# Sixteen first tiles and fifteen routing-query tiles as three products of rounded parts, and the router's gate shares taken between its index sums

## What is computed

```
# first stack, each layer l
h = rms_norm(x, attn_norm_g[l])
proj = h @ w_in[l]                    # 8932 columns: attention, rwkv, pool, retention, gates
r, wd, k, v, ad, gd = split_cols(token_shift(pb, mu), B_COLS)   # rwkv columns of proj
y = pooled(pc) @ pool_w                # pool columns of proj
...
x = x + square(relu(h2 @ mlp_up[l])) @ mlp_down[l]

# second stack, each layer l, after its mixer: PEER experts
q  = (h @ peer_w_q[l])                 # 2048 columns, 8 heads of 2 x 128
s  = q . sub_keys                      # 128 scores for each half of each head
top 16 of each half, top 16 of the 256 sums: the experts of a token and head
shares = softmax(the 16 sums)
out = sum over chosen experts of share * gelu(h . u_e) * v_e
```

## Time and profile before

| | |
|---|---|
| median of 3 runs | 4067.25 us (4060.14 to 4067.51) |
| the profiled execution's own time | 4059.76 us |
| its span, first to last instruction | 4057.9 us |
| PE busy | 96% of the span |
| DVE, ACT, POOL busy | 53%, 36%, 9% |
| mean granted clock of PE | 0.968 of full speed |

### The profile page before, as it was taken

The page is one execution under the profiler, slowest core; times in us unless marked ns, Lnnn a source line. Parts: engine busy times, 40 slices in busy tenths (PEclk is TensorE's granted clock), DMA queues, the critical chain, the costliest instruction groups (busy, mean ns, idle before and its releaser), DMA issues.

```text
span 4057.9 us, 65583 instructions
## 1 busy us (share of the span) xinstructions
PE 3881.6 (96%) x23880; PEld 3474.5 (86%) x23880; DVE 2157.3 (53%) x4800; ACT 1465.2 (36%) x3010; POOL 345.1 (9%) x468
## 2 busy tenths in 40 slices
PE   8999999999999999978999999999989999999999
PEld 6888889989888898776888989889878889898988
DVE  1345337523344474632697555555433985555555
ACT  2122126321211463212344444444432344444444
POOL 4001100040011000000044000000000270000000
PEclk9999999999899998978999999999999999999999
DMA  5552248654422585402423455555443325555453
GB/s 145 130 161 63 63 133 264 207 139 129 118 66 63 172 263 170 114 26 78 122 85 131 167 172 171 168 172 174 121 115 113 117 92 174 171 169 174 166 175 122
DMA packets 595489, 565.53 MB, mean 139 GB/s; under 512 B 56523, under 2 KB 520410, under 8 KB 594906
## 3 DMA queue, kind: packets, MB, share of 16 engines
q1 hardware_dynamic: 594660, 559.59, 45.5%
q0 software_dynamic: 352, 3.15, 0.2%
q10 hardware_dynamic: 278, 0.08, 0.0%
HBM read 553.30 MB, written 9.44 MB: 139 GB/s over the span
## 4 chain that ended last, share of the span: by engine, by line
PE 92%; DVE 5%; ACT 2%; issue 1%; SPq 0%; DMA 0%; DVEq 0%; ACTq 0%
PE bank L733 22%; PE bank L1187 14%; PE bank L753 10%; PE bank L1201 6%; PE bank L1202 6%; PE bank L1200 6%; PE bank L1139 5%; PE bank L1176 4%; PE bank L1154 3%; PE bank L729 2%; PE bank L822 1%; PE bank L1129 1%; PE bank L935 1%; PE bank L945 1%; PE bank L933 1%; PE bank L778 1%
## 5 line engine op out<-in xcount | busy, mean ns | idle before, releaser
L733 PE MATMUL bank<-hT,ring 128*128 128x256 f32 (+1 forms) x3184 | 716.6, 385 | 21.5 <-ACT hT L1426 16.2
L733 PEld LDWEIGHTS bank<-hT,ring 128*128 128x128 f32 (+1 forms) x3184 | 606.4, 191 | 115.7 <-issue 26.1
L1187 PE MATMUL bank<-h_high,u_parts 128*128 128x256 f32 x3072 | 437.9, 285 | 0.0
L2682 DVE TENSOR_TENSOR u_parts<-bank,u_parts 128x512 fp32r<-128x512 f32 x384 | 247.1, 685 | 328.4 <-ACT u_parts L1720 328.4
L1200 PE MATMUL bank<-v_high,w_low 128*128 128x512 f32 x1024 | 406.8, 397 | 0.4 <-DVE v_low L2703 0.4
L1201 PE MATMUL bank<-v_low,w_high 128*128 128x512 f32 x1024 | 406.1, 397 | 0.0
L1202 PE MATMUL bank<-v_high,w_high 128*128 128x512 f32 x1024 | 405.0, 396 | 0.0
L1187 PEld LDWEIGHTS bank<-h_high,u_parts 128*128 128x128 f32 x3072 | 395.5, 189 | 5.9
L1416 ACT ACTIVATE arena<-bank 128x256 f32<-128x256 f32 (+2 forms) x326 | 124.7, 386 | 684.5 <-PE bank L733 518.2
L2703 DVE TENSOR_TENSOR v_low<-ring,v_high 128x512 fp32r<-128x512 f32 x512 | 336.9, 689 | 65.5 <-ACT v_high L1737 41.3
L1720 ACT ACTIVATE u_parts<-bank 128x512 fp32r<-128x512 f32 x384 | 207.2, 591 | 352.8 <-PE bank L1187 347.0
(11 more groups left out here) (398 smaller groups left out, 5940.3 us busy)
## 6 DMA issues: line engine op xcount, KB each, us to landing
ring<-in_peer_u SPq DMA_DIRECT2D x256, 512.0 KB, 4.2
ring<-in_peer_v SPq DMA_DIRECT2D x256, 512.0 KB, 3.5
ring<-in_w_in SPq DMA_DIRECT2D x132, 512.0 KB, 3.8
ring<-in_mlp_up SPq DMA_DIRECT2D x64, 512.0 KB, 4.4
uT<-in_mod_w SPq DMA_DIRECT2D x64, 512.0 KB, 5.1
ring<-in_mlp_down SPq DMA_DIRECT2D x64, 512.0 KB, 4.6
ring<-in_w_branch SPq DMA_DIRECT2D x64, 256.0 KB, 2.8
ring<-in_mod_w SPq DMA_DIRECT2D x32, 512.0 KB, 4.5
```

The lines of the kernel that those rows point to most:

```text
L733: ins = eng.matmul(ps[0:n, 0:width], wv[:, i, :], moving(u * 8 + i), start=(u == 0 and i == 0), stop=(u == count - 1 and i == k - 1))
L1187: ins = eng.matmul(PB[6 + b][:, 0:S], u_parts[:, part, k * P:k * P + P], moving[:, k, :], start=(n == 0), stop=(n == len(products) - 1))
L2682: tt_(u_parts[:, 1, d], PB[4 + q][:, :], u_parts[:, 0, d].bitcast(F32), ALU.subtract).then_inc(sem("uL_ready"), 1)
```

## The change

1. The 16 full tiles of `first_tiles` (sk, sr, sv, pc) in both layers of the first stack, and tiles pq 1 to 15 in both layers of the second, go through `stream_split` with rounded parts. The three narrow tiles and pq 0 stay as they are. That is 2 x 16 + 2 x 15 = 62 tiles.
2. ACT rounds the hidden activations once more for each of these stages (`rounded_hidden`) and every weight unit; DVE takes the remainders. ACT calls `weights_high` for a tile in the tile's own turn, so the first unit of each stage is rounded after the tile before it (sgd, or pq 0) is copied out.
3. In layer 0 the angles, sines and cosines, which stood ahead of the first tiles on DVE and ACT, are spread between the first six of them; POOL, which waits for the angles, starts later, and its `condition` moves behind `means`.
4. In the router the logits are made at once in each half, ACT's exponential is asked for after the 21st early gelu instead of after the 24th, and the shares are made between the two index sums of the second half. Two one-element copies that only carried a semaphore go away.

```
+        IN_PARTS = ("up", "down", "sk", "sr", "sv", "pc", "pq")
+        PLAIN = {"pq": [(l, 0) for l in range(DEPTH)]}
...
+        first_weight_high = rounded("first_weight_high", "arena", 0, [P, HIGH, 1024])
+        first_high, first_low = rounded("first_high", "uT", 0, [P, KD, S]), rounded("first_low", "arena", 30112, [P, KD, S])
+        second_low = rounded("second_low", "arena", 27904, [P, KD, S])
...
+        FIRST_ANGLES, FIRST_SINES = (("sk", 0, 0), ("sk", 0, 1)), (("sk", 0, 2), ("sk", 0, 3))
+        FIRST_COSINES = (("sr", 0, 0), ("sr", 0, 1))
...
                 for j in range(16):
-                    stream(("pq", l, j), hidden)
+                    if j:
+                        stream_split(("pq", l, j), hidden_high, second_low, ("hidden_high", "hidden_split") if j == 1 else (None, None))
+                    else:
+                        stream(("pq", l, j), hidden)
...
                 for label in first_tiles(l):
-                    project(label)
+                    if in_parts(label):
+                        stream_split(label, first_high, first_low,
+                                     ("hidden_high", "hidden_split") if label == ("sk", l, 0) else (None, None))
+                    else:
+                        project(label)
...
+            def rounded_hidden(norm, high):
+
+                for k in range(KD):
+                    eng.wait_ge(sem("h_ready"), KD * norm + k + 1)
+                    eng.activation(high[:, k, :], hT[:, k, :], ACT.Copy).then_inc(sem("hidden_high"), 1)
...
-                end = min(split_end(label) + HIGH - 1, split_end(("down", label[1], KD - 1)))
+                end = min(split_end(label) + HIGH - 1, split_end(last_in_parts(label)))
...
                 for j in range(16):
+                    if j:
+                        weights_high(("pq", l, j))
                     evac(("pq", l, j), pq_t[:, j, :])
...
+                    if n == EARLY_ROUTER - 4:
+                        eng.wait_ge(sem("gate_logits"), act.next("gate_logits"))
+                        eng.activation(cv, cv, ACT.Exp).then_inc(sem("gate_exp"), 1)
...
-                    sines(0)
-                    sines(1)
+                rounded_hidden(2 * l, first_high)
                 for label in first_tiles(l):
+                    if in_parts(label):
+                        weights_high(label)
+                    if l == 0 and label in FIRST_SINES:
+                        sines(FIRST_SINES.index(label))
                     projected(label)
...
-                condition()
                 shift(l)
                 means(l)
+                condition()
...
+                split_hidden(first_high, first_low)
+                for label in first_tiles(l):
+                    if in_parts(label):
+                        weights_low(label)
...
+                        if t == TT - 1 and i == 0:
+                            shares()
...
+                split_hidden(hidden_high, second_low)
+                for j in range(1, 16):
+                    weights_low(("pq", l, j))
                 router(l)
```

More of the change, by code:

```diff
@@ L360, in two_stacks, with in_parts, last_in_parts @@
             unit_full.append(loads_in_slot[n % RING])
+        def in_parts(label):
+            return label[0] in IN_PARTS and label[1:] not in PLAIN.get(label[0], ())
+        def last_in_parts(label):
+            for kinds in (("sk", "sr", "sv", "pc"), ("up", "down"), ("pq",)):
+                if label[0] in kinds:
+                    return [x for x in tiles if x[0] in kinds and x[1] == label[1]][-1]
         split_units = [u for label, (_, first, count, _) in tiles.items()
-                       if label[0] in ("up", "down") for u in range(first, first + count)]
+                       if in_parts(label) for u in range(first, first + count)]
         split_at = {u: q for q, u in enumerate(split_units)}
+        first_units = {u for u in split_units for label in tiles if label[0] in ("sk", "sr", "sv", "pc")
+                       and tiles[label][1] == u}
+        mlp_at = {}
+        for l in range(DEPTH):
+            mlp = [u for label, (_, first, count, _) in tiles.items()
+                   if label[0] in ("up", "down") and label[1] == l for u in range(first, first + count)]
+            mlp_at.update((u, (l, q)) for q, u in enumerate(mlp))
         def split_end(label):
@@ L1786, in _ @@
                 root(rstd)
-                for k in range(KD):
-                    eng.wait_ge(sem("h_ready"), KD * (2 * l + 1) + k + 1)
-                    eng.activation(hidden_high[:, k, :], hT[:, k, :], ACT.Copy).then_inc(sem("hidden_high"), 1)
+                rounded_hidden(2 * l + 1, hidden_high)
                 for j in range(DFF // P):
@@ L2405, in weights_low @@
             def weights_low(label):
-                end = min(split_end(label) + HIGH - 2, split_end(("down", label[1], KD - 1)))
+                end = min(split_end(label) + HIGH - 2, split_end(last_in_parts(label)))
                 for q in range(low_made[0], end):
@@ L2747, in _ @@
                     eng.wait_ge(sem("dve_step"), dve.next("dve_step"))
-                    angles(0, "att", 0, 0)
-                    angles(1, "ret", 1, 0)
-                    for i in range(2):
-                        cosine(i)
+                split_hidden(first_high, first_low)
+                for label in first_tiles(l):
+                    if in_parts(label):
+                        weights_low(label)
+                    if l == 0 and label in FIRST_ANGLES:
+                        i = FIRST_ANGLES.index(label)
+                        angles(i, ("att", "ret")[i], i, 0)
+                    if l == 0 and label in FIRST_COSINES:
+                        cosine(FIRST_COSINES.index(label))
                 rwkv_prep(l)
```

73 lines of the change are left out of this document (38 added, 35 removed).

## The result

The changed kernel took 4039.15 us (median of 4 runs, 4032.24 to 4043.92), the kernel before 4067.38 beside it: ratio 0.9937, 95% interval [0.9921, 0.9952]. Timed once more beside more runs it took 4037.94 (5 runs) to 4068.91 (17 runs), 0.9927 [0.9914, 0.9941]. So the gain is 28 to 31 us; the forecast was 4046, with 17.4 us for the sum. The two profiled executions differ by less: 4057.9 of span before, 4039.1 after, 18.8 us. Why the two comparisons disagree turned out to be as useful to learn as the change itself.

A forecast was written before the change was run, and what follows sets the result against it. PE, busy 96%, was taken as the bound. Tiles -35.5, pauses +12.3, clock +9.2 and router -3.4 sum to -17.4 us; halfway between 4042.4 and 4049.9 gives 4046, 8-in-10 range 4034 to 4058.

The forecast's parts named there:

- What bounds it: Whole kernel: PE, busy 96% of the span, sets the pace; ACT and DVE work beside it is free.
- The tiles: 62 tiles in both stacks go from 3.453 to 2.880 us each: 35.5 us less.
- the same shape already runs in three products in the MLP: The MLP's 27 tiles at 2.880 us each were taken as the price of the newly converted tiles.
- The pauses: Four new PE waits at stage starts for copy, rounding and subtraction: 3 x 2.95 + 3.4 = 12.3 us more.
- the extra half microsecond: Layer 0, second stack: ACT's eight roundings delay the copy of pq 0, making that pause 3.4 us, elsewhere 2.95.
- The clock behind the pauses: PE runs at half clock after each of the four new pauses: 2.3 us each, 9.2 us more.
- light pauses: Rival, chance 0.17: the clock holds through 3 us pauses, the 9.2 goes, sum -26.6, time 4037.
- The router: PE's waits for the picked columns shorten by 1.72 us in each layer: 3.4 us less; ACT does not stall on logits.
- POOL: Rival, chance 0.06: in the first stack DVE's subtractions wait for POOL's instructions, 16.3 us lost, time 4062.
- the prediction's point of 3.44 us a unit: First-stack tile time above which the rival of DVE's subtractions colliding with POOL would decide.

The follow-up runs named there:

- a0_again: The changed kernel run and profiled once more, unaltered: 4037.94 us.
- e2_pause_a: Changed kernel, but PE waits at the start of each of the four stages for the second low weight instead of the first: 4047.24 us.
- e3_pause_b: Changed kernel, but PE waits at the start of each of the four stages for the third low weight instead of the first: 4056.63 us.
- e8_shift72: Changed kernel with both moving operands of the routing-query tiles 72 elements (288 bytes) further on: 4028.30 us, run once.
- e10_offsets: Changed kernel with moving operands of MLP and routing queries 288 bytes off the weights' place within 1024 bytes, except the up tiles' low part: 4030.00 us.
- e11_best: Changed kernel with each stage's first weights prepared ahead, so no pause at the four starts, plus the operand shifts of e10_offsets: 4010.66 us.

## Why the prediction was right, and where it was off

**What bounds it.** Right. PE stayed at 96%, and ACT's and DVE's new work between the tiles was hidden: in the four stages PE waited for a subtraction only at the start.

**The tiles: 35.5 forecast, 37.7 measured (37.2 in a0_again).** The 30 query tiles run at 2.880 us, exactly the MLP's price. The 32 tiles of the first stack run at 2.813 (2.827 in a0_again), so 20.5 us there in place of 18.3. The step that was off is "the same shape already runs in three products in the MLP": same shape, but not the same places in memory, and in the first stack these are worth about 2%.

**The pauses: 12.3 forecast, 11.1 measured.** The chain was right. In layer 0 of the second stack ACT's eight roundings took 2.54 us and not 3.3, and were over 0.3 us before the copy of pq 0; the extra half microsecond did not come.

**The clock behind the pauses: 9.2 forecast, 1.6 and 0 measured in the changed kernel's two profiles, 2.6 in the mean of six.** This is the term that was mis-sized, and it alone made the forecast gain some 7 us too small. I chose 2.3 us a pause because one of 1.83 us had been followed by half clock. The runs give, for dense products after a pause of 2.7 to 2.9 us, no loss in 18 of 28 cases, 1.4 to 1.7 us in eight and 3 us in two. From 3.85 us on they give 1.4 to 2.8 us every time. So what the prediction had as the cost of each pause is that of about one in three, and even behind pauses of 4 us dense products lost less than the earlier trace rows suggested. The rival "light pauses" is nearer to the mechanism, though not a rule, and its 4037 lies within 2 us of both medians. For that it needed its base as well: its sum of -26.6 is still 2 to 4 us short of the medians' -28.2 and -31.0.

The Trainium skill, page "TensorE: Matmul & The Clock Gate", section "Why this matters for your kernels", warns of idle gaps of PE between bursts of matmuls. The prediction took it to speak against light pauses. But the page means gaps a little longer than the 2.7 to 2.9 us that PE stood here, so on pauses of this length it gives no such warning. The traces agree with it from 3.85 us on. Below that length they go further than the page: 10 of the 28 shorter gaps were followed by half clock too.

**The router: 3.4 forecast, 3.4 measured alone and 4.3 and 4.0 in the whole.** ACT took its exponential at 2048.57 straight behind its 21st gelu, without waiting for the logits, and DVE found it done; its sums of the shares followed the first index sum without a gap:

```profile
2051.81 0.29 DVE L2661 TENSOR_REDUCE arena<-arena 128x8 f32<-128x128 f32 x1
...
2061.53 0.88 PE L1153 MATMUL bank<-cst,arena 128*128 128x128 f32 x6 [1.71 <-DVE arena L2706]
```

**POOL.** The overlap costs both engines time, and nearly all of it is hidden. Of the first stack's 32 subtractions eleven took 1.41 to 2.58 us in place of the 1.22 of the earlier trace rows, all eleven while an instruction of POOL's ran; none of the 158 elsewhere took over 1.23. Not every overlap is dear: others beside POOL took 1.22 to 1.23. POOL's own instruction of 128x256 went from 926 to 1379 ns in the mean:

```profile
840.89 2.13 DVE L2460 TENSOR_TENSOR weight_low<-ring,first_weight_high 128x1024 fp32r<-128x1024 f32 x1 [1.59 <-ACT first_weight_high L1626]
...
L1940 POOL TENSOR_SCALAR arena<-arena,vec 128x256 f32<-128x256 f32 x24 | 32.7, 1379 | 0.6
```

One does show, at the pause of layer 1 in the first stack. Its one subtraction ran beside POOL:

```profile
826.33 0.93 POOL L1940 TENSOR_SCALAR arena<-arena,vec 96x256 f32<-96x256 f32 x1
826.45 1.42 DVE L2460 TENSOR_TENSOR weight_low<-ring,first_weight_high 128x1024 fp32r<-128x1024 f32 x1 [7.92 <-ACT first_weight_high L1626]
```

That is 0.20 us over the 1.22, and the pause was 2.92 us and not 2.72. The second subtraction there took 1.75, and with both of them ahead of PE, in e2_pause_a and e3_pause_b, this pause was 0.73 us longer than the others' 3.85 and 4.99. In the row at 840.89 DVE still idled 1.59 us before its subtraction and the tiles kept their 2.813 us, so the prediction's point of 3.44 us a unit (worked out again from its own sum, 3.42) was never near.

The Trainium skill, page "SBUF — State Buffer", section "Who interferes with whom", has a DVE instruction with two SBUF inputs contend with a GpSimd instruction that reads SBUF. This case's traces fit: the subtraction has both its inputs in SBUF, and only beside POOL did it take longer. That the shared port is the reason is the page's account; no run here took POOL's work away to show it.

**The whole.** With the measured terms the sum is -37.7 + 11.1 + 1.5 - 4.3 = -29.4, and the medians gave -28.2 and -31.0. So the forecast gain of 17.4 was 12 us too small, and the four terms erred the same way: 2.2 in the tiles, 1.2 in the pauses, 7.7 in the clock, 0.9 in the router. That 4046 lay within 7 us of the result owes something to luck with the base: I took the middle between a profiled execution at 4059.76 and a median of 4067.25, which belong to the two heaps. From the median alone the same sum would have said 4049.9. The range had a slip of its own: with 1.6 us a pause and the lower base the working gives 4039.6, not 4038.

## What to carry to other kernels

Where a stage starts with work that must be prepared, prepare its first unit behind the stage before: here that was a handful of lines and 8 to 10 us. Measure the pace of an already converted stage, but look where its operands lie before calling it the price of the new one. Compare profiled executions by stages and with the granted clock beside them: the two of this study differed by 10 us in a stretch that the change never touched, a third of what there was to find. And count a rare event over every profile at hand: two said that one short pause in eight costs clock, eight said one in three.

## What was not expected of the hardware

- Three products of rounded parts, 128x256 a matmul, run at 0.933 to 0.96 us a group of eight with PE busy throughout and at full clock, depending on how the operands lie in SBUF. Shifting all by 288 bytes leaves 0.94 and 0.96; shifting the moving operands against the rest by 288 bytes gives 2.80 to 2.83 us a tile for 2.88, by 640 bytes 2.85. Which pair does it stays open.
- The place is not all. At unchanged places the first stack's groups ran 0.938 us apart in one execution of the changed kernel and 0.942 in the other, the queries' 0.933 in layer 0 and 0.942 in layer 1 of e8_shift72 and e10_offsets but 0.933 in both of e11_best, and the down tiles' went from 0.933 to 0.942 in the middle of a stage. What tips it was not found. The 0.96 never moved.
- Retention's sparse products of layer 0 ran through at 2.4 GHz in six profiles and at 1.2 in eight, for 20 us. The same stage in layer 1 was at half clock in all fourteen. What tips it in layer 0 was not found.
- PE's pauses ahead of dense products were followed by half clock in 10 of 28 cases at 2.7 to 2.9 us, most often at one place (6 of 7) and never at another (0 of 7), and in eight of eight at 3.85 to 5.7 us.
